# Second-layer attention of a fused two-block kernel: heads in pairs, two pairs of score banks, later divisions and turns

## What is computed

```python
def gqa_softmax(qg, k, v):
    s = jnp.einsum('bqgrd,bkgd->bgrqk', qg, k, preferred_element_type=jnp.float32) * (HEAD_DIM ** -0.5)
    p = jax.nn.softmax(s, axis=-1).astype(v.dtype)
    return jnp.einsum('bgrqk,bkgd->bqgrd', p, v)
...
        mx = jnp.concatenate([
            latent_attention(q, k, v, kc, vc),
            pool_mix(zx[..., KV_END:POOL_END], w_pool[i], pool_scale[i]),
            fourier_mix(zx[..., POOL_END:], w_four[i]),
        ], axis=-1)
        x = x + ga1 * (mx @ w_out[i])
```

## Time and profile before

| What | Value |
|---|---|
| runs | 1560.25 us median of 3 (1559.68 to 1561.62) |
| profiled execution, its own time | 1558.64 us |
| its span | 1556.8 us |
| TensorE busy | 1381.8 us (89%) |
| VectorE, ScalarE busy | 715.1 us (46%), 487.2 us (31%) |
| mean granted TensorE clock | 0.948 |
| the stage of layer 1's attention | 659.97 to 709.15 us of the span |

### The profile page before, as it was taken

The page is one execution under the profiler, slowest core; times in us unless marked ns, Lnnn a source line. Parts: engine busy times, 40 slices in busy tenths (PEclk is TensorE's granted clock), DMA queues, the critical chain, the costliest instruction groups (busy, mean ns, idle before and its releaser), DMA issues.

```text
span 1556.8 us, 24705 instructions
## 1 busy us (share of the span) xinstructions
PE 1381.8 (89%) x10342; PEld 1045.2 (67%) x10342; DVE 715.1 (46%) x1337; ACT 487.2 (31%) x933; POOL 31.5 (2%) x29
## 2 busy tenths in 40 slices
PE   7999999999999999999999999999886766676564
PEld 4764668778777777848999999998653333343332
DVE  4546565555555655556656568676421011110101
ACT  3436433222122223455444544564310000000001
POOL 0000010000000010001000000000000000000000
PEclk9999999999999999979999999999999789787878
DMA  9728618555663662705565329335999999999996
GB/s 358 279 85 255 229 55 310 180 203 189 222 236 123 232 196 85 216 1 193 183 213 183 126 74 324 106 118 210 389 425 425 426 425 426 426 426 425 426 425 267
DMA packets 164171, 393.01 MB, mean 252 GB/s; under 512 B 11588, under 2 KB 124760, under 8 KB 134360
## 3 DMA queue, kind: packets, MB, share of 16 engines
q1 hardware_dynamic: 163336, 389.88, 66.9%
q10 hardware_dynamic: 720, 1.49, 0.3%
HBM read 390.29 MB, written 1.05 MB: 251 GB/s over the span
## 4 chain that ended last, share of the span: by engine, by line
PE 70%; DMA 24%; DVE 2%; ACT 2%; issue 1%; SPq 1%; DVEq 0%; ACTq 0%
DMA R<-in_w_dram 22%; PE ps L1003 16%; PE ps L1004 15%; PE ps L1009 15%; PE ps L3057 3%; PE ps L1031 2%; PE ps L1025 2%; PE ps L1026 2%; PE ps L632 2%; PE ps L1413 1%; PE ps L1511 1%; PE ps L1349 1%; PE ps L3107 1%; SPq L416 1%; DMA R<-in_w_in_dram 1%
## 5 line engine op out<-in xcount | busy, mean ns | idle before, releaser
L969 DVE TENSOR_TENSOR WL<-R,WH 128x1024 fp32r<-128x1024 f32 (+1 forms) x202 | 225.2, 1129 | 132.4 <-ACT WH L959 132.3
L3057 PE MATMUL ps<-R,XG 128*32 128x256 f32 x2048 | 168.8, 487 | 123.6 <-DMA R<-in_w_dram 117.7
L1003 PE MATMUL ps<-HH,WH 128*128 128x256 f32 (+2 forms) x872 | 272.3, 333 | 0.0
L1004 PE MATMUL ps<-HL,WH 128*128 128x256 f32 (+2 forms) x872 | 268.9, 330 | 0.0
L959 ACT ACTIVATE WH<-R 128x1024 fp32r<-128x1024 f32 (+1 forms) x202 | 191.2, 961 | 152.9 <-PE ps L1009 113.5
L3057 PEld LDWEIGHTS ps<-R,XG 128*32 128x32 f32 x2048 | 87.0, 135 | 200.1 <-issue 182.1
L1003 PEld LDWEIGHTS ps<-HH,WH 128*128 128x128 f32 (+1 forms) x872 | 163.5, 188 | 24.6 <-issue 4.7
L1004 PEld LDWEIGHTS ps<-HL,WH 128*128 128x128 f32 (+1 forms) x872 | 163.2, 187 | 16.3
L1009 PE MATMUL ps<-HH,WL 128*128 128x256 f32 (+2 forms) x872 | 164.7, 331 | 0.0
L1003 PE MATMUL ps<-GH,WH 128*128 128x512 f32 (+1 forms) x480 | 154.0, 339 | 1.0 <-DVE MU L1791 1.0
L1004 PE MATMUL ps<-GL,WH 128*128 128x512 f32 (+1 forms) x480 | 153.4, 339 | 0.0
(11 more groups left out here) (497 smaller groups left out, 1701.2 us busy)
## 6 DMA issues: line engine op xcount, KB each, us to landing
R<-in_w_dram SPq DMA_DIRECT2D x192, 1024.0 KB, 26.5
R<-in_w_ada_dram SPq DMA_DIRECT2D x72, 1024.0 KB, 7.1
R<-in_w_gate_up_dram SPq DMA_DIRECT2D x40, 1024.0 KB, 7.9
R<-in_w_in_dram SPq DMA_DIRECT2D x20, 1024.0 KB, 9.9
R<-in_w_down_dram SPq DMA_DIRECT2D x16, 768.0 KB, 4.3
R<-in_w_down_dram SPq DMA_DIRECT2D x16, 640.0 KB, 4.2
R<-in_w_in_dram SPq DMA_DIRECT2D x8, 512.0 KB, 7.1
R<-in_w_out_dram SPq DMA_DIRECT2D x16, 256.0 KB, 5.5
```

The costliest lines, as they stand in the source:

```text
L969: last = e.tensor_tensor(L, w, H.bitcast(F32), ALU.subtract)
L1003: e.matmul(b[0:n, 0:N], H[:, k, 0:n], xh(k, N), start=(k == order[0]), stop=False)
L1004: e.matmul(b[0:n, 0:N], H[:, k, 0:n], xl(k, N), start=False, stop=False)
L3057: mm = e.matmul(PS[4][32 * g:32 * g + 32, 0:256], x[:, 4 * hf + k, :], w[g // 2][:, k, 256 * (g % 2):256 * (g % 2) + 256], start=(hf == 0 ...
```

## The change

1. The score banks become two pairs, (0, 1) and (5, 7). A step x is now a pair of heads, 8 in all: both score matmuls stand next to each other, then the two turns of pair x - 2 (LAG = 2).
2. On VectorE both maxima of pair x come first, then both divisions of pair x - 1.
3. The copies of the turned pair x - 2 stand behind both exponentials of pair x on ScalarE.
4. The last rows that are folded go to bank 3, which was the output bank of the last projection tile, in place of bank 7.
5. The mixers move from bank 5 to bank 4, which they share with the values; the last one takes bank 0. MIX_AT, `value_at`, the waits on those banks, LAST_OUTS and LAST_ORDER follow; the last mixer stands between the last turns and the last values.

```diff
-    LAST_ORDER = (4, 5, 0, 1, 6, 2, 7, 3)
+    LAST_ORDER = (4, 5, 0, 6, 1, 2, 7, 3)
...
+    def folded_bank(i, j):
+        return PS[3] if i and j else PS[7]
...
+        elif i:
+            e.wait_ge(*bank_out(1, 3))
...
-        if A == 2 and m:
-            e.wait_ge(s_gl, out_index(2, m - 1) + 1)
-        elif A < 2 and (m >= 2 or A == 1):
+        if A == 2:
+            e.wait_ge(*(mix_free(1, 1, 0), mix_free(1, 2, 0), (s_gl, out_index(2, 1) + 1), (s_gl, out_index(2, 2) + 1))[m])
+        elif m >= 2 or A == 1:
...
-    SCORE_BANKS = (0, 1, 7)
-    LAG = 3
-    MIX_AT = {2: 0, 6: 1, 10: 2, 17: 3}
+    SCORE_BANKS = ((0, 1), (5, 7))
+    LAG = 2
+    MIX_AT = {1: 0, 3: 1, 5: 2, 9: 3}
...
+        if x >= 2:
+            e.wait_ge(s_ex, 32 + 2 * x - 2)
+        elif x == 1:
+            e.wait_ge(s_zf, 11)
+            e.wait_ge(s_rope, 30)
...
+        for g in range(2):
+            r = slice(64 * g, 64 * g + 64)
+            e.matmul(score_bank(x, g)[:, :], QT[r, m, 128 * a:128 * a + 128], KTr[r, :], start=True, stop=True).then_inc(s_sco, 1)
...
+        for x in range(11):
+            if x < 8:
                 pe_last_scores(e, x)
-            if x == 1:
+            if x == 0:
                 pe_folded(e, 1, 1, 0)
+            if LAG <= x < 8 + LAG:
+                pe_last_turn(e, x - LAG)
+            if value_at(x) is not None:
+                pe_values(e, 2, value_at(x))
             if x in MIX_AT:
                 pe_last_mixer(e, MIX_AT[x])
...
+            if x < 8:
+                for g in range(2):
+                    dve_last_max(e, x, g)
+            if 1 <= x < 9:
+                for g in range(2):
+                    dve_divide(e, 2, x - 1, g)
...
-        return PS[5] if i else PS[mix_index(0, x, S) % 4]
+        if i:
+            return PS[0] if x == 3 else PS[4]
+        return PS[mix_index(0, x, S) % 4]
...
+        elif x == 1:
+            e.wait_ge(*mix_free(1, 0, 0))
+        elif x == 2:
+            e.wait_ge(s_gl, out_index(2, 0) + 1)
         else:
-            e.wait_ge(*mix_free(1, x - 1, 0))
+            e.wait_ge(s_ex, 46)
```

More of the change, by code:

```diff
@@ L1143, in folded_count @@
         return 11 + j if i else 2 + 2 * j + st
+    def folded_bank(i, j):
+        return PS[3] if i and j else PS[7]
     def pe_folded(e, i, j, st):
         e.wait_ge(s_evi, 10 * i + 8 + j + 1)
+        bank = folded_bank(i, j)
         if j == 0 and st == 0:
             e.wait_ge(s_z, 3 * i + 3)
+        elif i:
+            e.wait_ge(*bank_out(1, 3))
         else:
@@ L1152, in pe_folded @@
             c = 256 * st + odd
-            last = e.matmul(PS[7][:, 256 * odd:256 * odd + 256], ZT[j][:, c:c + 255:2], CSW[:, j, :], start=True, stop=True)
+            last = e.matmul(bank[:, 256 * odd:256 * odd + 256], ZT[j][:, c:c + 255:2], CSW[:, j, :], start=True, stop=True)
         last.then_inc(s_ztr, 1)
@@ L1157, in act_folded @@
         e.wait_ge(s_ztr, folded_turned(i, j, st))
-        e.activation(ZF[j][:, st, :, :], PS[7][:, :].rearrange("p (r n) -> p r n", r=2), ACT.Copy).then_inc(s_zf, 1)
+        e.activation(ZF[j][:, st, :, :], folded_bank(i, j)[:, :].rearrange("p (r n) -> p r n", r=2), ACT.Copy).then_inc(s_zf, 1)
     def dve_rows(e, i, j):
@@ L1389, in act_turned @@
                      ACT.Copy).then_inc(s_pt, 1)
-    LAST_OUTS = (("pool", 0), ("pool", 1), ("value", 0), ("value", 1), ("four", 0), ("value", 2), ("four", 1), ("value", 3))
+    LAST_OUTS = (("pool", 0), ("pool", 1), ("value", 0), ("four", 0), ("value", 1), ("value", 2), ("four", 1), ("value", 3))
     def out_index(A, m):
@@ L1487, in dve_value_low, with score_bank @@
             .then_inc(s_gl, 1)
-    SCORE_BANKS = (0, 1, 7)
-    LAG = 3
-    MIX_AT = {2: 0, 6: 1, 10: 2, 17: 3}
+    SCORE_BANKS = ((0, 1), (5, 7))
+    LAG = 2
+    MIX_AT = {1: 0, 3: 1, 5: 2, 9: 3}
     def value_at(x):
-        return (x - 7) // 4 if 7 <= x < 20 and (x - 7) % 4 == 0 else None
-    def head_at(x):
-        return x // 4, x // 2 % 2, x % 2
+        return (x - 4) // 2 if 4 <= x < 11 and x % 2 == 0 else None
+    def score_bank(x, g):
+        return PS[SCORE_BANKS[x % 2][g]]
@@ L1500, in pe_last_scores @@
     def pe_last_scores(e, x):
-        m, a, g = head_at(x)
-        if a == 0 and g == 0:
+        m, a = x // 2, x % 2
+        if a == 0:
             e.wait_ge(s_rope, 15 + 3 * (m + 2))
[L1504 to L1507, removed]
-        else:
-            e.wait_ge(*bank_out(1, x))
-        r = slice(64 * g, 64 * g + 64)
-        e.matmul(PS[SCORE_BANKS[x % 3]][:, :], QT[r, m, 128 * a:128 * a + 128], KTr[r, :], start=True, stop=True).then_inc(s_sco, 1)
@@ L1519, in act_last_exp, with dve_last_max @@
+    def dve_last_max(e, x, g):
+        v = 32 + 2 * x + g
+        e.wait_ge(s_sco, v + 1)
+        e.tensor_reduce(stats(v)[:, 0:1], score_bank(x, g)[:, :], AX.X, ALU.max, negate=True).then_inc(s_max, 1)
+    def act_last_exp(e, x, g):
+        v = 32 + 2 * x + g
         e.wait_ge(s_max, v + 1)
         e.wait_ge(s_tn, v - 3)
-        e.activation(P1[v % 4][:, :], PS[SCORE_BANKS[x % 3]][:, :], ACT.Exp, bias=stats(v)[:, 0:1], accum_out=stats(v)[:, 1:2])\
+        e.activation(P1[v % 4][:, :], score_bank(x, g)[:, :], ACT.Exp, bias=stats(v)[:, 0:1], accum_out=stats(v)[:, 1:2])\
@@ L1522, in act_last_exp @@
             .then_inc(s_ex, 1)
     def pe_last_turn(e, x):
[L1525 to L1533, removed]
+        for g in range(2):
+            v = 32 + 2 * x + g
+            e.wait_ge(s_nrm, v + 1)
+            if x:
+                e.wait_ge(s_pt, v - 1)
+            elif g:
+                e.wait_ge(s_zf, 12)
+            else:
+                e.wait_ge(*bank_out(1, 2))
+            for j in range(4):
+                last = e.transpose(PS[2 + g][:, 128 * j:128 * j + 128], P1[v % 4][:, 128 * j:128 * j + 128], ident)
+            last.then_inc(s_tn, 1)
@@ L1535, in pe_last_attention @@
     def pe_last_attention(e):
-        for x in range(20):
-            if x < 16:
+        for x in range(11):
+            if x < 8:
                 pe_last_scores(e, x)
-            if x == 1:
+            if x == 0:
                 pe_folded(e, 1, 1, 0)
+            if LAG <= x < 8 + LAG:
+                pe_last_turn(e, x - LAG)
+            if value_at(x) is not None:
+                pe_values(e, 2, value_at(x))
             if x in MIX_AT:
                 pe_last_mixer(e, MIX_AT[x])
[L1543 to L1546, removed]
@@ L1548, in act_last_attention @@
     def act_last_attention(e):
[L1549 to L1552, removed]
+        for x in range(11):
+            if MIX_AT.get(x - 1, 0) >= 2:
+                act_four_out(e, 1, MIX_AT[x - 1] - 2, 0)
+            if x < 8:
+                for g in range(2):
+                    act_last_exp(e, x, g)
+            if x == 0:
                 act_folded(e, 1, 1, 0)
-            if 3 <= x < 19:
-                act_turned(e, 2, (x - LAG) // 2, (x - LAG) % 2)
@@ L1559, in act_last_attention @@
                 act_value_out(e, 2, value_at(x))
+            if LAG <= x < 8 + LAG:
+                for g in range(2):
+                    act_turned(e, 2, x - LAG, g)
             if MIX_AT.get(x, 0) >= 2:
                 act_four_odd(e, 1, MIX_AT[x] - 2, 0)
-            if MIX_AT.get(x - 1, 0) >= 2:
-                act_four_out(e, 1, MIX_AT[x - 1] - 2, 0)
-            if x == 13:
+            if x == 7:
                 act_split(e, first_of["out", 1])
     def dve_last_attention(e):
[L1568 to L1572, removed]
+        for x in range(11):
+            if MIX_AT.get(x - 1, 0) >= 2:
+                dve_four_low(e, 1, MIX_AT[x - 1] - 2, 0)
+            if x < 8:
+                for g in range(2):
+                    dve_last_max(e, x, g)
+            if 1 <= x < 9:
+                for g in range(2):
+                    dve_divide(e, 2, x - 1, g)
+            if MIX_AT.get(x, 2) < 2:
+                dve_pool_low(e, 1, MIX_AT[x], 0)
+            if value_at(x) is not None:
+                dve_value_low(e, 2, value_at(x))
             if MIX_AT.get(x, 0) >= 2:
                 dve_four_sum(e, 1, MIX_AT[x] - 2, 0)
[L1575 to L1581, removed]
+            if x == 8:
                 dve_split(e, first_of["out", 1])
@@ L1723, in block_program @@
         bank_free[t] = mix_free(0, x, S)
-        bank_free[first_of["out", 1] + j] = (s_pt, 48)
+        last = first_of["out", 1] + j
+        bank_free[last] = (s_pt, 48) if tiles[last].bank else mix_free(1, 3, 0)
     def pe_mixer(e, i, x, S):
```

7 lines of the change are left out of this document (2 added, 5 removed).

## The result

| | before | after |
|---|---|---|
| median of the runs | 1560.93 us (1559.68 to 1565.24, 4 runs) | 1547.3 us (1543.09 to 1547.85, 4 runs) |
| ratio to before | | 0.9904, 95% interval 0.9887 to 0.9922 |
| profiled execution, its own time | 1558.64 us | 1547.85 us |
| its span | 1556.8 us | 1546.0 us |
| the stage, first scores to `out` | 49.2 us | 37.8 us |

What follows compares the result with a forecast made beforehand. TensorE's layer 1 attention stage (49.2 us) was taken to bind, its savings reaching the end. Scores -7.3, turns -1.1, waits +0.5, clock -7.7 give -15.6, rounded to 15.5: 1560.25 - 15.5 = 1544.8 us, range 1541 to 1551.

Steps and rivals of the forecast that it cites:

- Side by side: Layer 1 attention on TensorE: two heads' scores cost what one costs, 1.06 us; scores save 7.3, turns 1.1.
- The clock, early: Clock of 0.50 from 667 to 684 us, behind the idle 2.46, goes away: -7.7 us.
- The waits: TensorE's idle time in the stage: 1.4 + 0.8 + 1.9 + 0.9 = 5.0 against 4.5, so +0.5 us.
- late items of VectorE: Behind pair 7, VectorE late by the values' remainder: 0.3 us, within a wait of 1.9.
- the forecasts of 1.4, 0.8, 1.5 and 0.9: Waits ahead of mixer 0, at pair 1, ahead of pair 6's turn (from 1.9 split 0.4 and 1.5), before the last turns.
- the second weak place: The 1.9 us of waits late in the stage; a short fall of the clock there costs 1 to 2 us.
- signs of being wrong: Clock 0.50 for more than 4 us, TensorE idle over 7 us in the stage, or stage shrinks and end does not.
- Rival A: Clock still falls early in the stage, since turns may be weak support: 1551.7 us; chance 0.14.
- Rival B: Loop through three engines binds, nothing overlaps: stage 46.7 us, time 1557.7; chance 0.03.
- rival D: Waits keep TensorE at 1.2 GHz for the whole stage: slower by 5 us, 1565; chance 0.04.
- Rival C: Loads hide the saving, as the stream behind 1100 us does not depend on compute: 1560 us; chance 0.03.
- At nothing: Folded rows in bank 3, shared bank 4, last mixer in bank 0, LAST_ORDER and two us less load lead cost nothing.

Runs made afterwards that it cites:

- heads apart: Changed kernel, from the third pair on with scores and turn of head 0, then of head 1: 1552.9 us, ratio 0.9958.
- bank 7: Changed kernel with the last folded rows back in bank 7, so the second pair's scores wait for their copy: 1549.26 us, ratio 0.9928.
- the moved outputs: Changed kernel with the Fourier mixer's two outputs behind the next pair's exponentials, maxima and divisions: 1545.95 us, ratio 0.9902.
- the moved divisions: Changed kernel with each pair's divisions directly behind its own maxima on VectorE: 1548.91 us, ratio 0.9923.

## Why the prediction was right, and where it was off

- **The total.** Forecast 1544.8 with a range of 1541 to 1551, measured 1547.3 and 1544.2 in two sessions. That the number fits so well is in part luck: the profiled execution was forecast at 1543.1 and took 1547.85 (2.5 for the late fall, 1.6 for the rest of the stage, 0.7 near the end), and the medians fell by 13.6 and 17.2 us where the stage gives 11.4, or 13.9 without the late fall. No trace shows where the medians gained the rest.
- **Side by side.** Right. A pair costs 1.06. The scores and turns were to save 7.3 + 1.1; of these the experiment that put six of the pairs apart took back 5.7 us, net of waits.
- **The clock, early.** The price of 7.7 us held: the kernel before with the idle time filled has a stage of 41.5. That the fall would go was right too, in both profiles of the changed kernel. The reason was incomplete. In the traces it takes both the shorter idle time and the pairs: 1.4 us of idle time ahead of single heads still let the clock fall (heads apart), and so did 2.46 ahead of pairs (bank 7). There the clock came back in under 4 us, not 17.
- **The waits.** Off: forecast 5.0, measured 6.1, and the work of TensorE about 0.5 longer (35.3 against 33.7 at full clock). The step that failed is the one on late items of VectorE. I let it be 0.3 us late behind pair 7; but the maxima of pair 6 had stood 1.6 us behind their scores, queued behind the Fourier mixer's remainder, which waited for ScalarE. The wait of 0.70 on pair 5 followed, where I had 0.4: with the outputs moved it was gone and the stage 0.6 shorter. The wait on pair 2 (0.29, where I had 0) is not from there, since it stayed, and its cause is open. The forecasts of 1.4, 0.8, 1.5 and 0.9 were 1.40, 0.96, 1.69 and 1.09.
- **The late fall.** Named as the second weak place, with a cost of 1 to 2 us, but left out of the sum. It costs 2.5 us and is present in both profiled executions of the changed kernel. With it and the 1.6 above, -15.5 becomes -11.4, the stage in the profile.
- **The signs.** One of the prediction's own signs of being wrong came true: the clock stood at 0.50 for some 6 us (687 to 693), where more than 4 was to count against it. The stage (37.8, not 33 to 35) and the start of the DMA stream (11.5 us earlier, not 15) missed as well, all for the same late fall and the longer waits. The idle time of 6.1 stayed under 7, and the end moved with the stage.
- **Rival A (early fall kept).** Did not occur in the profiles of the changed kernel; it did in the profile with heads apart, and five of that kernel's 12 times lie in the group of that profile. By the rule of the Trainium skill in "TensorE: Matmul & The Clock Gate", Part 4, that transposes do not count as busy time in the same way, the sum would have been nearer to 1551.7; the measurement decides against that sum. Whether transposes count less was not tested by itself.
- **Rival B** (one serial loop, stage 46.7 us) and **rival D** (low clock throughout): the stage of 37.8 rules both out. **Rival C** (hidden by the loads): the load stream began 11.5 us earlier and the end came 10.8 earlier.
- **At nothing.** The bank changes cost nothing, and the one in bank 3 saves 1.06 us of idle time and, by it, a short fall of 1.6 us (scores 2.01 for 1.06, turns 1.52 for 1.02, mixer 0.84 for 0.70). The earlier use of the loads cost nothing: from `out` to the load named above it is 376.6 us as before.

What stays open: the changed kernel's faster group was not caught in a trace, so what sets it apart is not known, and one run of the kernel before at 1550.07, among others of 1557 to 1565, may be one in which the early fall was missing; no trace shows it.

## What to carry to other kernels

Put matmuls that use different halves of the contraction rows next to each other; with a transpose between them each head costs its full 1.05 us again. Price an idle gap of TensorE by what stands behind it too: a gap of 1.4 us cost only itself with pairs behind it, and some 8 us more in the profile where single heads followed. Before attacking the engine that the profile names for a wait, look when the second latest condition is met; it was equally late here.

## What the runs showed of the hardware that I had not expected

Six matmuls that compute nothing took 9.7 us off the median of the kernel before (1561.4 to 1551.7, ratio 0.9941); 7.7 of them are the stage, in which TensorE then stays at 2.4 GHz. Two heads side by side cost what one costs at 1.2 GHz too (2.0 us). Whether a gap lets the clock fall is not fixed by its length: ahead of the turns of pair 6, 1.69 us did in three profiles (the changed kernel twice, bank 7), and 1.69 and 1.74 us in two others did not (the moved outputs, the moved divisions), with the same turns and values behind it. And the clock also fell without any gap, behind matmuls of 4 contraction rows, in seven of the thirteen profiles, for 1.6 us each. The same program falls into groups of times 3 us (changed kernel) or 8 us (heads apart) from each other; the falls are of that size, but that they alone make the groups is argued, not shown.
